# Forgetting attention: two row maxima and the normalisation ahead of the last state steps, three weight blocks behind them, and the last state group's inputs in two pairs

## The chip, the cores and the metric

One core of one Trainium2 chip runs the whole program. The metric is device time in microseconds of one execution. All matrix work is on the tensor engine (PE), vector arithmetic on the vector engine (DVE), activations and many copies on the scalar engine (ACT), and the sync engine (SP) issues the DMA transfers. Every engine works through its own list of instructions in order, and waits on semaphores.

## What the reference computes

The program is a chain of four transformer layers over 256 tokens of width 1024. The change touches the mixer of the third, which runs a softmax attention with forgetting (8 heads of 64) beside a state space scan (S5, width 512), and multiplies both by one output matrix:

```python
def fox_s5_mixer(x, w_in, f_bias, ..., d_skip, w_glu, b_glu, w_out):
    z = x @ w_in
    q, k, v, f_logit, u = jnp.split(z, ...)
    att = forgetting_attention(q, k, v, f_logit + f_bias)     # softmax(q k^T/8 + c_i - c_j) v
    y = s5_scan(u, ..., d_skip)                               # complex scan, then C h + d_skip * u
    y = jax.nn.gelu(y)
    y = y * jax.nn.sigmoid(y @ w_glu + b_glu)
    return jnp.concatenate([att, y], axis=-1) @ w_out
```

Behind it come a residual, a layer norm, and a mixture of experts.

## The kernel before, in words

**Weights.** Matrices come in pieces of 128 by 1024 floats (512 KB), numbered through the program. SP loads piece n into one of four raw slots, and waits for that until the low part of piece n-4 is made. ACT copies it, rounded, to a high slot (`hi_to(n)`, one CAST of WH from WR; there are five such slots), and DVE makes the remainder (`lo_to(n)`, one TENSOR_TENSOR of WL from WR and WH). The order of ACT and DVE work around these is written out by hand: `filled(u)` first makes pieces up to three beyond the one in use, then waits for a PSUM bank.

The stage "fox" has pieces 0 to 23 of its own: 0 to 15 are input weights, 16 to 23 the rows of `w_out`. When they are named here by number, the count is from `FIRST["fox"]`. `down(s, ...)` multiplies the activations GH/GL of row block s with piece 16+s into four banks, 12 matmuls. Blocks 0 to 3 are the attention's, 4 to 7 the state part's.

**Attention.** There are 16 units (head, query tile), i = 0 to 15. For each PE scores into a bank, DVE takes the maximum of the rows (L2664), ACT the exponential (L1465), PE transposes it (`turn`, L882), ACT copies that back (`keep_turned`, L1556), and PE multiplies with the values (`fox_value`). Behind unit 15 DVE normalises (`normalize_out`, L2408 and two products), PE transposes the result (`turn_out`, L892), and ACT and DVE split it into GH and GL (`high_out`, `low_out`).

**State part.** Four groups i = 0 to 3. `s5_in(i)` on PE makes the inputs of a group in four banks (two pairs), which ACT copies (L1730, L1731). DVE turns them by an angle, scans and turns them back, in the generator `s5_states`: seven steps a group, 28 in all, each taken by one `next(states)`. The steps of a group are: the two products with the cosine; the first sine product and sum; the second sine product and difference, with the skip term (`s5_skip`) of the group before; four scans; four scans; two products into RS and ACC; two into AR, which signal `s_grot`. `s5_out(i)` on PE waits for that signal and makes the group's output.

**The end of the stage.** `s5_skip` adds d_skip * u to an output. ACT applies gelu to groups 0 to 2 in one instruction, makes the high parts up to piece 23, and applies gelu to group 3. PE multiplies with the gate's weights (`gate_units`): groups 0 to 2 first, group 3 (8 matmuls) behind it. ACT takes the sigmoid, DVE multiplies, ACT and DVE split into GH and GL, and PE runs the blocks 4 to 7 (`down_by_tiles`).

**Banks.** Scores, state inputs and outputs take turns in a ring of four PSUM banks, in the order of PE's program. A bank is taken again once its last reader is through.

Of the kernel before, what the change touches and what calls it, by code (L numbers as in the profile page):

```python
# [21 lines left out]
LOOK = 3  # L22
# [114 lines left out]
PLAN, FIRST = weight_plan()  # L137
# [225 lines left out]
def build(nc, a, out):  # L363
    ctx = ExitStack()
    with ctx:
# [124 lines left out]
        GLB, at = {}, 0  # L490
# [45 lines left out]
        fot = AR[:, r.at + 256:r.at + 1280]  # L536
# [101 lines left out]
        def _(e):  # L638
# [111 lines left out]
                half_of_tokens(u, 0)  # L750
                half_of_tokens(u, 1)

            def down(i, made, first, last, bank_of=lambda b: 4 + b):

                n, h, l = piece()
                e.wait_ge(s_gl.sem, made)
                for b in range(4):
                    ts, fs = slice(b // 2 * P, b // 2 * P + P), slice(b % 2 * 512, b % 2 * 512 + 512)
                    t = mm3(bank(bank_of(b)), gh[:, i, ts], gl[:, i, ts], h[:, fs], l[:, fs], first, last)
                    if last:  # L760
                        t.then_inc(s_y.sem, 1)
                if not last:
                    t.then_inc(s_used.sem, 1)
# [374 lines left out]
                e.wait_ge(s_t2.sem, 8 * STAGE["fox"] + k + 1)  # L1138
                t = mm(bank(u.b, 0, 256, p=8), foxg[:, k, :], t2[:, k, :], k == 0, k == 7)
            t.then_inc(u.fill[0], 1)  # L1140
            def s5_in(i):
                for pair in range(2):
                    us = [use(("s5b", i, 2 * pair + x)) for x in range(2)]
                    for r in range(2):
                        for x, u in enumerate(us):
                            rows = slice(64 * pair + 32 * x, 64 * pair + 32 * x + 32)
                            t = mm(bank(u.b, r * 256, r * 256 + 256), BT[r][rows, i, :], fuf[rows, i, :], True, True)
                            if r:
                                t.then_inc(u.fill[0], 1)
# [41 lines left out]

            fox_scores(0)
            for i in range(18):
                if i in (4, 11):
                    s5_in(2 + i // 7)
                if i < 15:
                    fox_scores(i + 1)
                if i >= 2:
                    if (i - 2) % 8 == 0:
                        e.wait_ge(*ring.uses["fv", (i - 2) // 8].free)  # L1200
                    fox_value(i - 2)
                if 1 <= i <= 16:
                    turn(16 + i - 1, fSb[(i - 1) % 3], (i - 1) % 2 + 1, (s_exp.sem, 16 + i))
                if i == 0:
                    features(("fq", 1), "fox")
                if i == 2:
                    features(("fk", 1), "fox")
                if i == 5:
                    tokens(("fv", 1))
                if i in (3, 9, 15):  # L1210
                    s5_out((i - 3) // 6)
            busy(3)
            turn_out("fox", fot, 4)
            busy(4)

# [7 lines left out]
                    if 3 in ks:  # L1223
                        t.then_inc(u.fill[0], 1)

            for s in range(2):
                down(s, GLB["fox"] + 1, s == 0, False)
            us = [use(("glu", s)) for s in range(2)]
            e.wait_ge(s_glu.sem, 32)
            e.wait_ge(s_ys.sem, 1)  # L1230
            gate_units(us, range(3))
            down(2, GLB["fox"] + 2, False, False)
            s5_out(3)
            down(3, GLB["fox"] + 2, False, False)
            e.wait_ge(s_ys.sem, 2)
            gate_units(us, [3])
            down_by_tiles(range(4, 8), [GLB["fox"] + 3 + x // 2 for x in range(4)], True)
            layer_norm_and_logits(0)

# [218 lines left out]
        def _(e):  # L1458
# [262 lines left out]
                A.wait()  # L1721
                A(act(x, x, ACTF.Ln, bias=1.0), s_lsa)

            def s5_in(i):
                for jj in range(4):
                    u = ring.uses["s5b", i, jj]
                    filled(u)
                    if i and jj == 0:
                        e.wait_ge(s_s5r.sem, i)
                    e.copy(Br[:, jj, :], bank(u.b, 0, 256))  # L1730
                    A.frees(e.copy(Bi[:, jj, :], bank(u.b, 256, 512)), u)  # L1731
# [36 lines left out]
            for i in range(17):  # L1768
                if i < 16:
# [6 lines left out]
                    if i >= 3:  # L1776
                        e.wait_ge(*pring.uses["pt", 16 + i - 3].fill)
                    A(act(sbf, bank(u.b, 0, n), ACTF.Exp, bias=mx[:, c:c + 1], accum=den[:, c:c + 1]), s_exp)
                if i in (4, 11):
                    s5_in(2 + i // 7)  # L1780
                if i:
                    keep_turned(16 + i - 1, (i - 1) % 2 + 1, fpts[(i - 1) % 2], 16 + i - 2)
                if i == 0:
# [198 lines left out]
        def _(e):  # L1982
# [628 lines left out]
            V(ts(fcf, fcw, -1.0, None, ALU.mult), s_cpos)  # L2611
            def s5_skip(i):
                u = ring.uses["s5y", i]
                filled(u)
                V.frees(stt(YS[:, i, :], fuf[:, i, :], par("s5d", i, 1), bank(u.b, 0, 256), ALU.mult, ALU.add), u)

            def s5_states():
# [41 lines left out]
            for i in range(16):  # L2659
# [2 lines left out]
                u = ring.uses["fs", i]  # L2662
                filled(u)
                V(e.tensor_reduce(mx[:, c:c + 1], bank(u.b, 0, n), AX.X, ALU.max, negate=True), s_neg)  # L2664
                next(states, None)
            lo_to(FIRST["fox"] + 18)
            next(states, None)
            normalize_out(fot, 32)
            lo_to(FIRST["fox"] + 19)
            low_out("fox")  # L2670
            next(states, None)
            next(states, None)
            for n in range(FIRST["fox"] + 20, FIRST["fox"] + 23):
                next(states, None)
                lo_to(n)
            for _ in states:
                pass
            lo_to(FIRST["fox"] + 23)
            s5_skip(3)
            for s in range(2):  # L2680
                lo_to(ring.uses["glu", s].piece + LOOK)
                e.wait_ge(*ring.uses["glu", s].free)
                V(tt(fqf[:, 2 * s:2 * s + 2, :], fqf[:, 2 * s:2 * s + 2, :], YS[:, 2 * s:2 * s + 2, :], ALU.mult), s_glum)
                low_of(GLB["fox"] + 3 + s, 4 + 2 * s, 6 + 2 * s, fqf[:, 2 * s:2 * s + 2, :])
# [495 lines left out]
```

## Time and profile before

| what | value |
|---|---|
| three runs, median (lowest to highest) | 1477.95 us (1476.88 to 1481.66) |
| the profiled execution, its own time | 1481.88 us |
| its span in the trace | 1480.1 us |
| PE busy | 1412.4 us, 95% |
| DVE busy | 1172.9 us, 79% |
| ACT busy | 827.7 us, 56% |

The shares of busy time are averages over stages of very different kinds. The stretch that the change touches lies between 838 and 900 us of the span. How long something took there, and what ended each wait, is read from the order of instructions in time.

### The profile page before, as it was taken

The numbers are of one execution on the slowest core, as the hardware profiler recorded it, in microseconds if no ns is written. First come the engines' busy times: TensorE is split into PE (matmuls) and PEld (weight loads), VectorE is DVE, ScalarE is ACT, GpSimd is POOL, SyncE is SP. The second block draws the span as 40 slices with busy tenths as digits, with TensorE's granted clock in tenths as the row PEclk, the third lists the DMA queues.
The fourth block names the chain that finished last, engine by engine and source line by source line (L and its number), as shares of the span: only waits on it lengthen the run. The fifth ranks groups of instructions, "written<-read, shape, count | busy, mean of one in ns | idle before, by whom it ended". The sixth has DMA issues, their size and how long they took to land.

```text
span 1480.1 us, 22953 instructions
## 1 busy us (share of the span) xinstructions
PE 1412.4 (95%) x8738; PEld 1245.1 (84%) x8738; DVE 1172.9 (79%) x1800; ACT 827.7 (56%) x1210; POOL 1.2 (0%) x5
## 2 busy tenths in 40 slices
PE   7889899999999999999999889999999999999997
PEld 7888788888898979999979668888879998888886
DVE  4898787887865757598569887799988966879997
ACT  1442444544544445444676435788866564678874
POOL 0000000000000000000000000000000000000000
PEclk7899999999999999999999999999999999999999
DMA  9973389997575524655735124899954544589992
GB/s 367 323 297 108 122 307 345 342 331 255 180 227 163 187 70 143 199 180 180 212 111 147 58 92 179 301 384 368 385 197 115 165 121 156 180 322 374 372 380 78
DMA packets 184480, 333.76 MB, mean 225 GB/s; under 512 B 13340, under 2 KB 127796, under 8 KB 184372
## 3 DMA queue, kind: packets, MB, share of 16 engines
q1 hardware_dynamic: 184372, 332.31, 64.7%
q8 instruction: 70, 1.15, 0.3%
q14 instruction: 38, 0.31, 0.1%
HBM read 331.18 MB, written 1.09 MB: 224 GB/s over the span
## 4 chain that ended last, share of the span: by engine, by line
PE 76%; DVE 13%; DMA 4%; ACT 3%; issue 3%; SPq 1%; DVEq 0%; ACTq 0%
PE PSA L645 14%; PE PSA L647 14%; PE PSA L646 14%; PE PSA L642 13%; PE PSB L645 5%; PE PSB L646 5%; PE PSB L647 5%; PE PSB L642 4%; DVE WL L1996 2%; DMA WR<-ffn_w_in 2%; DVE ACC L1993 2%; DVE T L1996 1%; DVE AR L1996 1%; DMA WR<-hyb_w_in 1%; ACT WH L1475 1%
## 5 line engine op out<-in xcount | busy, mean ns | idle before, releaser
L1996 DVE TENSOR_TENSOR WL<-WR,WH 128x1024 fp32r<-128x1024 f32 x352 | 422.4, 1219 | 100.4 <-ACT WH L1475 99.7
L1475 ACT CAST WH<-WR 128x1024 fp32r<-128x1024 f32 x352 | 357.0, 1048 | 114.4 <-DMA WR<-hyb_w_in 45.0
L645 PE MATMUL PSA<-XHL,WH 128*128 128x256 f32 x976 | 282.7, 290 | 8.4 <-ACT T L1464 2.2
L647 PE MATMUL PSA<-XHL,WL 128*128 128x256 f32 x976 | 277.1, 284 | 0.0
L646 PE MATMUL PSA<-XHL,WH 128*128 128x256 f32 x976 | 277.1, 284 | 0.0
L645 PEld LDWEIGHTS PSA<-XHL,WH 128*128 128x128 f32 x976 | 188.0, 193 | 13.9 <-issue 5.2
L1996 DVE TENSOR_TENSOR WL<-AR,WH 128x1024 fp32r<-128x1024 f32 x152 | 178.4, 1219 | 14.1 <-ACT WH L1475 14.1
L646 PEld LDWEIGHTS PSA<-XHL,WH 128*128 128x128 f32 x976 | 188.2, 193 | 0.9 <-issue 0.5
L647 PEld LDWEIGHTS PSA<-XHL,WL 128*128 128x128 f32 x976 | 188.1, 193 | 0.0
L645 PE MATMUL PSB<-WH,GH 128*128 128x512 f32 x400 | 159.5, 399 | 5.0 <-DVE GL L1996 5.0
L646 PE MATMUL PSB<-WL,GH 128*128 128x512 f32 x400 | 156.7, 392 | 0.0
L647 PE MATMUL PSB<-WH,GL 128*128 128x512 f32 x400 | 156.5, 391 | 0.0
L1475 ACT CAST WH<-AR 128x1024 fp32r<-128x1024 f32 x152 | 151.5, 1049 | 4.0 <-PE PSA L647 4.0
L642 PE MATMUL PSA<-XHL,WH 128*128 128x512 f32 x336 | 118.8, 397 | 2.1 <-ACT T L1464 1.6
L645 PE MATMUL PSA<-WH,XHL 128*128 128x256 f32 (+1 forms) x352 | 116.2, 330 | 3.9 <-DVE AR L1993 2.7
L647 PE MATMUL PSA<-WH,XHL 128*128 128x256 f32 (+1 forms) x352 | 113.5, 322 | 0.0
L646 PE MATMUL PSA<-WL,XHL 128*128 128x256 f32 (+1 forms) x352 | 113.3, 322 | 0.0
L645 PEld LDWEIGHTS PSB<-WH,GH 128*128 128x128 f32 x400 | 75.5, 189 | 23.9 <-issue 8.5
L642 PE MATMUL PSA<-XHL,WL 128*128 128x256 f32 x336 | 94.3, 281 | 0.0
L647 PEld LDWEIGHTS PSB<-WH,GL 128*128 128x128 f32 x400 | 75.5, 189 | 16.3
L646 PEld LDWEIGHTS PSB<-WL,GH 128*128 128x128 f32 x400 | 75.6, 189 | 15.1 <-issue 0.5
L1464 ACT ACTIVATE AR<-PSA 128x256 f32<-128x256 f32 (+1 forms) x71 | 31.1, 441 | 94.8 <-PE PSA L647 94.8
(276 smaller groups left out, 2372.4 us busy)
## 6 DMA issues: line engine op xcount, KB each, us to landing
AR<-moe_w_gate_up SPq DMA_DIRECT2D x96, 512.0 KB, 6.4
WR<-ffn_w_in SPq DMA_DIRECT2D x88, 512.0 KB, 4.9
WR<-moe_w_gate_up SPq DMA_DIRECT2D x64, 512.0 KB, 6.4
AR<-ada_w SPq DMA_DIRECT2D x59, 512.0 KB, 9.2
AR<-moe_w_down SPq DMA_DIRECT2D x56, 512.0 KB, 6.8
WR<-ffn_w_out SPq DMA_DIRECT2D x44, 512.0 KB, 4.2
WR<-att_w_qkv SPq DMA_DIRECT2D x36, 512.0 KB, 5.0
AD<-ada_w SPq DMA_DIRECT2D x34, 512.0 KB, 6.3
```

What stands on the lines that cost most here:

```text
L642: return e.matmul(o, l, r, start=start, stop=stop, skip_group_check=skip)
L645: e.matmul(o, lh, rh, start=start, stop=False, skip_group_check=True)
L646: e.matmul(o, lh, rl, start=False, stop=False, skip_group_check=True)
L647: return e.matmul(o, ll, rh, start=False, stop=stop, skip_group_check=True)
L1464: return e.activation(o, i, f, bias=bias, scale=scale)
L1475: A(e.copy(hi_slot(m), raw_slot(m)), s_hi)
L1993: return e.scalar_tensor_tensor(out=o, in0=i, scalar=s, in1=j, op0=op0, op1=op1)
L1996: return e.tensor_tensor(o, i, j, op)
```

## The change

It edits the programs of PE, ACT and DVE between unit 11 of this attention and the end of the stage.

```diff
 PE
-                if i in (4, 11):
-                    s5_in(2 + i // 7)
+                if i == 4:
+                    s5_in(2)
+                if i in (11, 12):
+                    s5_in(3, (i - 11,))
...
-                if i in (3, 9, 15):
+                if i in (3, 9):
                     s5_out((i - 3) // 6)
-            busy(3)
+            s5_out(2)
             turn_out("fox", fot, 4)
...
-            for s in range(2):
-                down(s, GLB["fox"] + 1, s == 0, False)
+            for s in range(3):
+                down(s, GLB["fox"] + 1 + s // 2, s == 0, False)
...
             gate_units(us, range(3))
-            down(2, GLB["fox"] + 2, False, False)
             s5_out(3)
-            down(3, GLB["fox"] + 2, False, False)
-            e.wait_ge(s_ys.sem, 2)
-            gate_units(us, [3])
+
+            def last_gate_units():
+                e.wait_ge(s_ys.sem, 2)
+                gate_units(us, [3])
+
+            down(3, GLB["fox"] + 2, False, False, between=last_gate_units)
 ACT
-                if i in (4, 11):
-                    s5_in(2 + i // 7)
+                if i == 4:
+                    s5_in(2)
+                if i in (11, 12):
+                    s5_in(3, (i - 11,))
 DVE
             def s5_skip(i):
                 u = ring.uses["s5y", i]
-                filled(u)
+                e.wait_ge(*u.fill)
...
-                next(states, None)
+                if i < 14:
+                    next(states)
+            next(states)
+            normalize_out(fot, 32)
             lo_to(FIRST["fox"] + 18)
-            next(states, None)
-            normalize_out(fot, 32)
-            lo_to(FIRST["fox"] + 19)
+            next(states)
             low_out("fox")
-            next(states, None)
-            next(states, None)
-            for n in range(FIRST["fox"] + 20, FIRST["fox"] + 23):
-                next(states, None)
-                lo_to(n)
             for _ in states:
                 pass
+            lo_to(FIRST["fox"] + 19)
+            s5_skip(3)
             lo_to(FIRST["fox"] + 23)
-            s5_skip(3)
             for s in range(2):
-                lo_to(ring.uses["glu", s].piece + LOOK)
```

The DVE list from the maximum of unit 14 to the low parts of the attention's result, as it stood. AR<-T,AR is the last step of group 2 (the one that signals `s_grot`), T<-T,AR and T<-T are the first steps of group 3, RECIPROCAL and AR<-PSB,SM are the normalisation:

```order
L2664 TENSOR_REDUCE SM<-PSA 128x1 [waits s_bank1_filled]
L1996 TENSOR_TENSOR AR<-T,AR 128x1024 [waits s_neg_made]
L1996 TENSOR_TENSOR AR<-T,AR 128x1024
L2664 TENSOR_REDUCE SM<-PSA 128x1 [waits s_bank2_filled]
L1996 TENSOR_TENSOR T<-T,AR 128x1024 [waits s_neg_made,s_bank2_free]
L1996 TENSOR_TENSOR T<-T,AR 128x1024 x2
L1996 TENSOR_TENSOR T<-T 128x1024 [waits s_dve_step]
L2408 RECIPROCAL SM<-SM 128x8 [waits s_exp_made]
L1996 TENSOR_TENSOR AR<-PSB,SM 128x512 [waits s_dve_step,s_val_made]
...
L1996 TENSOR_TENSOR WL<-WR,WH 128x1024 [waits s_hi_made]
L1996 TENSOR_TENSOR GL<-PSA,GH 128x512 [waits s_gh_made,s_bank0_filled]
```

And in the changed kernel (its lines are numbered eight higher):

```order
L2672 TENSOR_REDUCE SM<-PSA 128x1 [waits s_bank1_filled]
L2672 TENSOR_REDUCE SM<-PSA 128x1 [waits s_bank2_filled]
L2004 TENSOR_TENSOR AR<-T,AR 128x1024 [waits s_neg_made]
L2004 TENSOR_TENSOR AR<-T,AR 128x1024
L2416 RECIPROCAL SM<-SM 128x8 [waits s_exp_made]
L2004 TENSOR_TENSOR AR<-PSB,SM 128x512 [waits s_dve_step,s_val_made]
...
L2004 TENSOR_TENSOR T<-T,AR 128x1024 [waits s_ot_made,s_bank3_free]
L2004 TENSOR_TENSOR T<-T,AR 128x1024
L2004 TENSOR_TENSOR GL<-PSA,GH 128x512 [waits s_gh_made,s_bank0_filled]
```

The two maxima now follow each other, the normalisation has one step of the state part ahead of it instead of three, and the low part of piece 19 (WL) is gone from this place.

Further down the same list, from the scans of group 3 to the product with the sigmoid, as it stood. T<-AR,T are the scans, RS and ACC the last step but one, AR<-T,AR the last, and AR<-AR,PR,PSA is the skip term of group 3:

```order
L2002 SCALAR_TENSOR_TENSOR T<-AR,T 128x256 x7
L1996 TENSOR_TENSOR WL<-WR,WH 128x1024 [waits s_hi_made]
L1996 TENSOR_TENSOR RS<-T,AR 128x1024 [waits s_lo_made]
L1993 SCALAR_TENSOR_TENSOR ACC<-T,AR 128x1024
L1996 TENSOR_TENSOR WL<-WR,WH 128x1024 [waits s_hi_made]
L1996 TENSOR_TENSOR AR<-T,AR 128x1024 [waits s_lo_made]
L1996 TENSOR_TENSOR AR<-T,AR 128x1024
L1996 TENSOR_TENSOR WL<-WR,WH 128x1024 [waits s_hi_made] x2
L1993 SCALAR_TENSOR_TENSOR AR<-AR,PR,PSA 128x256 [waits s_bank0_filled]
L1996 TENSOR_TENSOR AR<-AR 128x512 [waits s_bank2_free]
```

And in the changed kernel:

```order
L2010 SCALAR_TENSOR_TENSOR T<-AR,T 128x256 x7
L2004 TENSOR_TENSOR RS<-T,AR 128x1024 [waits s_dve_step]
L2001 SCALAR_TENSOR_TENSOR ACC<-T,AR 128x1024
L2004 TENSOR_TENSOR AR<-T,AR 128x1024 [waits s_dve_step]
L2004 TENSOR_TENSOR AR<-T,AR 128x1024
L2004 TENSOR_TENSOR WL<-WR,WH 128x1024 [waits s_hi_made]
L2001 SCALAR_TENSOR_TENSOR AR<-AR,PR,PSA 128x256 [waits s_bank0_filled]
L2004 TENSOR_TENSOR WL<-WR,WH 128x1024 [waits s_hi_made] x4
L2004 TENSOR_TENSOR AR<-AR 128x512 [waits s_bank2_free]
```

The low parts of pieces 20 and 21 leave the middle of the steps, and one low part (now piece 19) stands between the last step and the skip term, with four behind it (20 to 23) instead of two ahead.

On PE the last block of the attention's rows, `down(3)`, is split around the gate's last products (PSA<-AR):

```order
-L645 MATMUL PSB<-WH,GH 128x512
-L646 MATMUL PSB<-WL,GH 128x512
-L647 MATMUL PSB<-WH,GL 128x512
-L645 MATMUL PSB<-WH,GH 128x512
-L646 MATMUL PSB<-WL,GH 128x512
-L647 MATMUL PSB<-WH,GL 128x512
 L642 MATMUL PSA<-AR 128x256 [waits s_ys_made]
 L642 MATMUL PSA<-AR 128x256 x3
+L645 MATMUL PSB<-WH,GH 128x512
+L646 MATMUL PSB<-WL,GH 128x512
```

Six of its twelve matmuls come behind the gate's products now.

## Rows read from the trace of the kernel before

**Rows 1.** The page: the span, and busy time by engine
```profile
span 1480.1 us, 22953 instructions
...
PE 1412.4 (95%) x8738; PEld 1245.1 (84%) x8738; DVE 1172.9 (79%) x1800; ACT 827.7 (56%) x1210; POOL 1.2 (0%) x5
```

**Rows 2.** Timeline of DVE: start us, us, instruction, [idle before <-releaser]
```profile
841.48 2.44 DVE L2002 TENSOR_TENSOR_SCAN T<-AR,T 128x256 f32<-128x256 f32 x4
845.50 0.29 DVE L2664 TENSOR_REDUCE SM<-PSA 128x1 f32<-128x128 f32 x1 [1.59 <-PE PSA L642]
...
850.77 0.28 DVE L2664 TENSOR_REDUCE SM<-PSA 128x1 f32<-128x128 f32 x1
...
853.36 0.42 DVE L2664 TENSOR_REDUCE SM<-PSA 128x1 f32<-128x256 f32 x1
853.89 3.50 DVE L1996 TENSOR_TENSOR T<-T,AR 128x1024 f32<-128x1024 f32 x3
...
859.76 0.69 DVE L1996 TENSOR_TENSOR AR<-PSB,SM 128x512 f32<-128x512 f32 x1
860.37 1.22 DVE L1996 TENSOR_TENSOR WL<-WR,WH 128x1024 fp32r<-128x1024 f32 x1
861.68 1.29 DVE L1996 TENSOR_TENSOR GL<-PSA,GH 128x512 fp32r<-128x512 f32 x2
```

**Rows 3.** Timeline of PE over the same stretch and the end of the stage
```profile
842.24 2.08 PE L642 MATMUL PSA<-AR,AD 32*128 32x256 f32 x8 [2.09 <-ACT AR L1465]
...
853.59 0.74 PE L642 MATMUL PSA<-RS,AD 128*32 128x256 f32 x8 [0.91 <-DVE AR L1996]
...
856.83 0.69 PE L642 MATMUL PSB<-AR 128*128 128x64 f32 x2
...
858.21 0.66 PE L642 MATMUL PSB<-AR 128*128 128x64 f32 x4 [0.46 <-ACT AR L1556]
...
860.05 1.11 PE L892 MATMUL PSA<-CT,AR 128*128 128x128 f32 x8
...
882.50 1.89 PE L642 MATMUL PSA<-AR 128*128 128x256 f32 x8
886.65 0.47 PE L645 MATMUL PSB<-WH,GH 128*128 128x512 f32 x1 [2.26 <-DVE GL L1996]
```

**Rows 4.** Timeline of DVE, the end of the state part
```profile
875.23 2.36 DVE L1996 TENSOR_TENSOR AR<-T,AR 128x1024 f32<-128x1024 f32 x2
...
879.78 0.47 DVE L1993 SCALAR_TENSOR_TENSOR AR<-AR,PR,PSA 128x256 f32<-128x256 f32 x1
```

**Rows 5.** Timeline of ACT, the end of the stage
```profile
880.29 0.42 ACT L1464 ACTIVATE AR<-AR 128x256 f32<-128x256 f32 x1 [2.86 <-DVE AR L1993]
880.73 1.28 ACT L1464 ACT_TABLE_LOAD   x1
883.56 1.70 ACT L1464 ACTIVATE AR<-PSA,PR 128x256 f32<-128x256 f32 x4 [1.55 <-PE PSA L642]
```

**Rows 6.** One line's DMA issues: time from issue to landing
```profile
DMA to landing us min/median/max: 3.4/4.2/4.7
```

**Rows 7.** DMA issues between 880 and 890 us: KB each, us to landing
```profile
WR<-moe_w_gate_up SPq DMA_DIRECT2D x4, 512.0 KB, 8.6
```

**Rows 8.** Timeline of ACT behind the stage: cast, table load, activation
```profile
913.17 1.05 ACT L1475 CAST WH<-WR 128x1024 fp32r<-128x1024 f32 x1
914.24 1.28 ACT L1464 ACT_TABLE_LOAD   x1
915.53 0.21 ACT L1464 ACTIVATE SM<-SM 128x8 f32<-128x8 f32 x1
```

**Rows 9.** PE alone by stretch: busy, granted clock, DMA share, GB/s
```profile
854.00:856.00 2.00, 2.00 (x27) 0.50 0.03 8
...
888.00:890.00 2.00, 2.00 (x7) 0.53 1.04 420
890.00:892.00 2.00, 2.00 (x7) 0.61 0.65 264
```

More of the change, by code:

```diff
@@ L751, in tokens, with down @@
                 half_of_tokens(u, 1)
-            def down(i, made, first, last, bank_of=lambda b: 4 + b):
+            def down(i, made, first, last, bank_of=lambda b: 4 + b, between=None):
                 n, h, l = piece()
@@ L757, in down @@
                 for b in range(4):
+                    if b == 2 and between:
+                        between()
                     ts, fs = slice(b // 2 * P, b // 2 * P + P), slice(b % 2 * 512, b % 2 * 512 + 512)
@@ L1140, in _, with s5_in @@
             t.then_inc(u.fill[0], 1)
-            def s5_in(i):
-                for pair in range(2):
+            def s5_in(i, pairs=(0, 1)):
+                for pair in pairs:
                     us = [use(("s5b", i, 2 * pair + x)) for x in range(2)]
@@ L1722, in log_sigmoid, with s5_in @@
                 A(act(x, x, ACTF.Ln, bias=1.0), s_lsa)
-            def s5_in(i):
-                for jj in range(4):
+            def s5_in(i, pairs=(0, 1)):
+                for jj in range(2 * pairs[0], 2 * pairs[-1] + 2):
                     u = ring.uses["s5b", i, jj]
```

## The prediction

> **What bounds the kernel now.** I read the page first: PE is busy for 95% of a span of 1480.1 us [rows 1], so all that a reordering can win is waiting time of PE, and only where nothing else makes it up. The trace in order of time then shows that the touched stretch is one of the few where PE is not the bound. From the row maxima to the output of state group 3 it is DVE's list that runs without a gap, and PE, ACT and DMA wait for it. Three places matter. Before the maximum of unit 12 DVE itself sat idle for 1.59 us, for scores of PE [rows 2], and PE had been held by the second pair of state inputs, 2.09 us, until an exponential of ACT freed a bank [rows 3]. Between the maximum of unit 15 at 853.36 and the end of the normalisation at 860.45 (859.76 + 0.69) DVE ran four long state instructions [rows 2]. And after the last step of group 3 (875.23 + 2.36 = 877.59 [rows 4]) comes the chain skip term, gelu, gate, sigmoid, product, GL, until PE starts the state rows of the output matrix at 886.65 after 2.26 us of idling [rows 3]. From there on PE has work in a row, so I take 886.65 as the time that must move: what lies behind it (sums, layer norm, the experts' loads, which wait for the sums) starts from it and moves along. What does not arrive at 886.65 is worth nothing.
>
> **Step 1, two pairs of inputs.** The scores of unit 12 no longer queue behind the second pair. They need a bank whose reader is the skip term of group 1, done just before the scans that start at 841.48. These scans end at 843.92, and the maximum can follow at once instead of at 845.50: 1.6 us off DVE's list [rows 2]. The second pair runs beside the next scans, and PE and ACT have slack there. The lower bound is 0 (the scores late for another reason).
>
> **Step 2, maxima and normalisation.** With step 1 the maximum of unit 14 starts at 850.77 - 1.6 = 849.2, that of unit 15 at 849.5, 3.9 us earlier than 853.36 [rows 2]. What ends the attention then is the ping-pong of exponential, transposition, copy and value product for units 14 and 15. It took from 853.36 to 858.87 (858.21 + 0.66), and the output of group 2 stood inside it with 3.24 us (853.59 to 856.83) [rows 2, 3], part of it beside the exponential. I put the last value product at 854.0, 4.5 us after the maximum, and the end of the normalisation at 854.6, against 860.45.
>
> **Step 3, what this meets.** The output of group 2 now starts behind the value products, at 854.0, and the transposition of the result queues behind it. It took 3.24 us before, at the lower of PE's clock levels (granted 0.50 from 854 to 856 [rows 9]); half of that, 1.6 us, is my estimate for the full level. So the transposition starts at 857.2 or 855.6, and GL follows 1.63 us behind its start (860.05 to 861.68) [rows 2, 3]: at 858.8 or 857.3, against 861.68. The step gains **2.9 to 4.4 us**. The pair of products that DVE does between normalisation and GL (two of 1.2 us) fits into this wait and is free.
>
> **Step 4, from GL to the last step of group 3.** Before: 861.68 to 877.59, 15.9 us [rows 2, 4]. Two low parts leave it (2 x 1.2 us, as WL at 860.37); two state products of the same size, which had stood ahead of the normalisation, enter it. The length stays at 15.9 us, so the last step ends 2.9 to 4.4 us earlier: at 874.7 or 873.2.
>
> **Step 5, what is given back.** Piece 19's low part is now made behind this step (1.2 us; the output of group 3 on PE covers it, since the skip term started 2.19 us after the last step also before, 877.59 to 879.78 [rows 4]). But the load of piece 23 waits for exactly that low part, and ACT must cast piece 23 before it may apply gelu to group 3. Before, that load had been issued some 16 us ahead, and only the skip term held ACT (the wait of 2.86 us [rows 5]). Now the gelu starts at: last step + 1.2 (low part) + landing + 1.05 (cast [rows 8]) + 0.1. Loads of these rows landed in 3.4 to 4.7 us, median 4.2 [rows 6]; I take 3.5, nearest to the low end, since nothing else is in flight then. That is 5.8 us behind the last step, against 880.29 - 877.59 = 2.7 before [rows 4, 5]: **3.1 us lost**, 4.3 with a landing of 4.7. The four low parts behind the skip term (4.6 us) end a little after the cast of piece 23, at 881, about when the first sigmoids are through, and cost nothing; if they ended later, the product would wait one for one.
>
> **Step 6, the split of down(3).** Before, gelu started at 880.29, the gate's last products only at 882.50, since PE had to finish twelve matmuls, and the sigmoid at 883.56; 886.65 is 3.09 us behind the sigmoid [rows 3, 5]. Now the gate can start with the end of gelu, and the sigmoid with the end of the table load: gelu 0.42, load 1.28, then 3.09, together 4.8 us instead of 6.36. **1.55 us gained.** Behind the gate six matmuls are left, inside that 3.09.
> A rule of the Trainium skill weighs on this step. Here a table load of 1.28 us is followed by its activation without a gap (914.24, then 915.53 [rows 8]). "ScalarE: Activation LUTs", section "What ACT_TABLE_LOAD costs", adds a drain of about 1.38 us to each switch; the load before was hidden by PE, and it is not now, so by the page the step would gain 0.2 us and the whole change 0.7. I go by the row.
>
> **Sum.** 2.9 to 4.4, less 3.1, plus 1.55: 1.35 to 2.85, and with the late landing 0.1 to 1.6. I take 2.1. The profiled execution's own time of 1481.88 would become 1479.8. It lies 3.9 above the median of the runs; on the median 1477.95 the same 2.1 gives **1475.8 us**. A measurement of this kernel can tell about 0.3% from no change, which is 4.4 us: the forecast is a gain too small to be told.
>
> **The rivals.**
> *Forecast* (0.55): 1475.8, its own range 1474.2 to 1477.8.
> *PE's clock stays up* (0.2). From 888 to 892 us the granted clock was 0.53 and 0.61 [rows 9], partly the lower level (1.2 GHz), after the wait of 2.26 us [rows 3]; that costs 2 x 0.47 + 2 x 0.39 = 1.7 us of PE's work. If the new order keeps the full level there and during the output of group 2, the gain is 4.4 - 3.1 + 1.55 + 1.7 = 4.55: 1473.4. For it: the last wait of PE may shrink. Against it: PE now also waits ahead of the output of group 3 and of the gate's last products, and waits of 0.91 and 2.26 us stood before the two slow stretches [rows 3]. By "TensorE: Matmul & The Clock Gate", section "What's actually happening", of the Trainium skill, idling sends the clock down, which speaks for the slow stretch staying; the trace agrees that it did so before.
> *Nothing arrives* (0.15). The scores of unit 12 are late anyway, the output of group 2 runs at the lower level and the load lands in 4.7 us: the gain of steps 1 to 3 is used up by step 5. 1478.
> *Piece 23 decides for the worse* (0.1), the case on the other side. Four loads of the same size, issued together, took 8.6 us [rows 7]. If this one took as long, gelu would start 5.1 us later than I put it: 2.1 - 5.1 = -3.0, 1481.0. The change turns into a loss from a landing of 5.6 us on. Against it: the queue is empty at that time.
>
> **How the numbers follow.** The predicted time is the forecast's. The range of 8 in 10 reaches from just under the faster case to beyond the case where nothing arrives, as the spread of the runs shown (1476.88 to 1481.66) also asks: 1472.6 to 1480.0. Faster by over 0.3% needs the faster case and a little more than its own size, 0.15; slower by over 0.3% needs more than the whole price of the last rival, 0.05; within 0.3% is the rest, 0.80.
>
> **What would show it.** Step 1: no idling of DVE before the maximum of unit 12. Step 2: the two last maxima back to back. Step 3: PE's output of group 2 right ahead of the transposition, GL 3 to 4 us earlier against the maximum of unit 11. Step 5: ACT's cast of piece 23 released by its DMA, right ahead of the last gelu. Step 6: sigmoid directly behind the table load. Wrong is the prediction if the cast does not wait, if the transposition waits for something else than the output of group 2, or if the gain at the state rows is lost in the experts' stage.

## The result

The changed kernel took 1487.6 us (median of 8 runs, 1485.56 to 1490.01), the kernel before beside it 1480.71 us (8 runs, 1476.88 to 1484.66). The ratio is 1.0045, with a 95% interval of 1.0031 to 1.0058: slower by 6.7 us, where 2.1 us faster was forecast. Every ratio below is that of a kernel's runs to those of the kernel before, and a number of microseconds said to be by the ratio is worked out from it. The profiled execution's span is 1487.9 us against 1480.1 [rows 1].

```profile
span 1487.9 us, 22941 instructions
...
PE 1419.8 (95%) x8732; PEld 1250.5 (84%) x8732; DVE 1173.1 (79%) x1800; ACT 827.2 (56%) x1210; POOL 1.2 (0%) x5
```

The shares are the same as before. The time in order has to be read. First the DVE of the changed kernel (start us, us, instruction, [idle before <-releaser]), from the first state steps of group 1 on. AR<-AR,PR,PSA is the skip term (the one at 821.29 of group 0, that at 885.04 of group 3), RS and ACC the last step but one of a group.

```profile
815.40 1.23 DVE L2004 TENSOR_TENSOR T<-T 128x1024 f32<-128x1024 f32 x1
821.29 0.48 DVE L2001 SCALAR_TENSOR_TENSOR AR<-AR,PR,PSA 128x256 f32<-128x256 f32 x1 [4.67 <-PE PSA L642]
821.69 2.35 DVE L2004 TENSOR_TENSOR WL<-WR,WH 128x1024 fp32r<-128x1024 f32 x2
...
828.53 0.42 DVE L2672 TENSOR_REDUCE SM<-PSA 128x1 f32<-128x256 f32 x1 [1.81 <-PE PSA L642]
...
837.31 0.42 DVE L2672 TENSOR_REDUCE SM<-PSA 128x1 f32<-128x256 f32 x1 [1.16 <-PE PSA L642]
...
851.23 0.27 DVE L2672 TENSOR_REDUCE SM<-PSA 128x1 f32<-128x128 f32 x1
...
854.36 0.42 DVE L2672 TENSOR_REDUCE SM<-PSA 128x1 f32<-128x256 f32 x1 [0.53 <-PE PSA L642]
...
858.10 0.42 DVE L2672 TENSOR_REDUCE SM<-PSA 128x1 f32<-128x256 f32 x1 [0.71 <-PE PSA L642]
...
866.84 1.29 DVE L2004 TENSOR_TENSOR GL<-PSA,GH 128x512 fp32r<-128x512 f32 x2 [1.39 <-ACT GH L1568]
...
880.54 2.36 DVE L2004 TENSOR_TENSOR AR<-T,AR 128x1024 f32<-128x1024 f32 x2
882.81 1.22 DVE L2004 TENSOR_TENSOR WL<-WR,WH 128x1024 fp32r<-128x1024 f32 x1
885.04 0.48 DVE L2001 SCALAR_TENSOR_TENSOR AR<-AR,PR,PSA 128x256 f32<-128x256 f32 x1 [1.01 <-PE PSA L642]
```

The same place in the kernel before, which the rows ahead of the prediction do not show:

```profile
813.82 2.35 DVE L1996 TENSOR_TENSOR WL<-WR,WH 128x1024 fp32r<-128x1024 f32 x2
818.58 0.48 DVE L1993 SCALAR_TENSOR_TENSOR AR<-AR,PR,PSA 128x256 f32<-128x256 f32 x1 [2.40 <-PE PSA L642]
```

Here a loss starts that the prediction does not have. The skip term of group 0 waits for an output of PE. Before, DVE made two low parts first and then idled 2.40 us; now it idles 4.67 us and makes the two low parts behind the wait. The place is far ahead of unit 11, where the part of the change that I costed begins: that the change lies between unit 11 and the end of the stage, and the touched stretch between 838 and 900 us, as was said ahead of the prediction, is wrong. It follows from one line of the diff, `filled(u)` turned into a bare wait in `s5_skip`, which serves all four groups. In the two lists of instructions the place reads, before and now:

```
L1996 TENSOR_TENSOR WL<-WR,WH 128x1024 [waits s_hi_made] x2
L1993 SCALAR_TENSOR_TENSOR AR<-AR,PR,PSA 128x256 [waits s_bank1_filled]

L2001 SCALAR_TENSOR_TENSOR AR<-AR,PR,PSA 128x256 [waits s_bank1_filled]
L2004 TENSOR_TENSOR WL<-WR,WH 128x1024 [waits s_hi_made] x2
```

PE of the changed kernel, at the inputs of group 2, the output of group 2, the transposition, the output of group 3, the gate's last products, the second half of `down(3)` and the first state rows:

```profile
824.84 2.08 PE L642 MATMUL PSA<-AR,AD 32*128 32x256 f32 x8 [2.55 <-ACT AR L1471]
...
862.18 1.08 PE L642 MATMUL PSA<-RS,AD 128*32 128x256 f32 x8
...
865.24 1.09 PE L894 MATMUL PSA<-CT,AR 128*128 128x128 f32 x8
...
883.05 0.64 PE L642 MATMUL PSA<-RS,AD 128*32 128x256 f32 x8 [1.60 <-DVE AR L2004]
...
889.46 3.78 PE L642 MATMUL PSA<-AR 128*128 128x256 f32 x8 [2.89 <-ACT AR L1470]
892.68 0.99 PE L645 MATMUL PSB<-WH,GH 128*128 128x512 f32 x1
...
895.50 0.47 PE L645 MATMUL PSB<-WH,GH 128*128 128x512 f32 x1
```

PE alone by stretch (us, busy, granted clock, DMA share, GB/s):

```profile
822.00:826.00 4.00, 1.45 (x10) 0.71 0.48 140
826.00:830.00 4.00, 4.00 (x20) 0.50 0.36 122
...
850.00:854.00 4.00, 4.00 (x16) 0.50 0.00 0
...
890.00:894.00 4.00, 4.00 (x11) 0.50 0.94 251
```

PE waited 2.55 us at the inputs of group 2, for the exponential of unit 4, whose maximum now stands behind the two low parts (823.96), and worked at its lower clock level (granted 0.50) from 826 to 830; a second such stretch lay at 850, and a third from 890, on the gate's products, which took 3.78 us instead of 1.89 [rows 3].

ACT of the changed kernel at the end of the stage:

```profile
888.04 1.05 ACT L1481 CAST WH<-WR 128x1024 fp32r<-128x1024 f32 x1 [11.97 <-DMA WR<-even_w_out]
888.99 0.41 ACT L1470 ACTIVATE AR<-AR 128x256 f32<-128x256 f32 x1
889.42 1.28 ACT L1470 ACT_TABLE_LOAD   x1
891.57 0.84 ACT L1470 ACTIVATE AR<-PSA,PR 128x256 f32<-128x256 f32 x2 [0.87 <-PE PSA L642]
```
SP's queue in the same kernel, where the load of piece 23 is issued:
```profile
884.06 0.34 SPq L2969 DMA_DIRECT2D WR<-even_w_out  x1
```

The load of piece 23, issued at 884.06 behind the low part of piece 19, held the cast until 888.04 and the gelu behind it, as forecast.

**One clock for all traces.** The skip term of group 0 starts when PE has finished the output that it waits for, and up to that output PE's list is the same in every kernel here. That time lies between 816.5 and 822.3 us in the profiled executions. I count everything behind it from it. The table gives what the traces show, in us: DVE's idle time ahead of that skip term, then the start of the maxima of units 7, 12 and 15, of GL, the end of the last state step, the skip term of group 3, its gelu, the first sigmoid, the first state rows on PE, and the first product of the residual (XT) on DVE. Each row is one execution, the profiled one. Where the last two maxima are one row of the trace, the second is counted back from its end.

| kernel | idle | max 7 | max 12 | max 15 | GL | last step ends | skip 3 | gelu | sigmoid | state rows | XT |
|---|---|---|---|---|---|---|---|---|---|---|---|
| before | 2.40 | 11.33 | 26.92 | 34.78 | 43.10 | 59.01 | 61.20 | 61.71 | 64.98 | 68.07 | 74.76 |
| changed | 4.67 | 16.02 | 29.94 | 36.81 | 45.55 | 61.61 | 63.75 | 67.70 | 70.28 | 74.21 | 79.26 |
| e1 | 2.42 | 11.33 | 25.25 | 32.15 | 40.89 | 56.95 | 59.08 | 62.72 | 65.30 | 68.82 | 73.88 |
| e2 | 4.67 | 14.90 | 30.49 | 38.35 | 46.66 | 62.57 | 64.76 | 65.27 | 68.54 | 71.63 | 76.71 |
| e3 | 2.40 | 11.33 | 25.25 | 33.72 | 42.03 | 57.94 | 60.13 | 60.64 | 63.87 | 66.96 | 73.60 |
| e4 | 2.40 | 11.33 | 25.25 | 31.32 | 38.56 | 54.63 | 56.77 | 57.28 | 61.85 | 64.94 | 72.53 |
| e5 | 2.42 | 11.33 | 25.25 | 32.06 | 40.79 | 56.85 | 58.99 | 59.50 | 61.43 | 66.14 | 72.70 |
| e6 | 4.69 | 15.82 | 30.43 | 38.30 | 47.89 | 63.80 | 65.99 | 66.50 | 69.73 | 72.82 | 79.51 |
| e7 | 2.42 | 11.33 | 25.24 | 32.09 | 40.82 | 56.88 | 59.02 | 59.54 | 62.81 | 66.17 | 72.73 |
| e8 | 2.42 | 11.33 | 26.92 | 32.54 | 39.66 | 55.72 | 57.86 | 62.01 | 64.48 | 68.40 | 73.49 |
| e9 | 4.67 | 13.60 | 29.19 | 37.05 | 45.36 | 61.28 | 63.47 | 63.97 | 67.22 | 70.31 | 76.96 |
| e10 | 2.40 | 11.33 | 25.25 | 32.16 | 40.90 | 56.96 | 59.10 | 59.62 | 61.53 | 65.11 | 70.19 |
| e11 | 2.42 | 11.32 | 25.24 | 31.32 | 39.46 | 55.51 | 57.65 | 58.17 | 60.08 | 63.67 | 68.74 |
| e12 | 2.40 | 11.34 | 25.25 | 30.69 | 40.86 | 56.91 | 59.06 | 59.57 | 61.48 | 65.07 | 70.13 |

The changed kernel is 16.02 - 11.33 = 4.69 us behind at the maximum of unit 7, has won 2.66 of them back at unit 15, and is 2.6 behind at the last state step. Between the skip term of group 3 and its gelu, where the load of piece 23 is waited for, it loses another 3.4, and at the state rows it is 74.21 - 68.07 = 6.14 behind. At XT it is 4.50 behind (79.26 - 74.76), because the state rows themselves took longer in the kernel before: 6.69 us from their start to XT, with a granted clock of 0.53 and 0.61 [rows 9], against 5.05. Of the 7.8 us between the two spans another 2.7 lie ahead of the skip term, where nothing differs in the lists, and 0.6 behind XT.

### The profile page after: what moved, and what is told of

The parts are those of the page before. It is cut to its first block, busy times and chain, and to the rows that moved or that the text cites. A ratio compares the mean times of both kernels' runs of the same rounds, so it can differ in the third digit from the quotient of the medians.

```text
span 1487.9 us, 22941 instructions
## 1 busy us (share of the span) xinstructions
PE 1419.8 (95%) x8732; PEld 1250.5 (84%) x8732; DVE 1173.1 (79%) x1800; ACT 827.2 (56%) x1210; POOL 1.2 (0%) x5
## 4 chain that ended last, share of the span: by engine, by line
PE 71%; DVE 15%; DMA 6%; ACT 4%; issue 4%; SPq 1%; DVEq 0%; ACTq 0%
PE PSA L645 13%; PE PSA L642 13%; PE PSA L647 12%; PE PSA L646 12%; PE PSB L645 5%; PE PSB L646 5%; PE PSB L647 5%; PE PSB L642 4%; DVE WL L2004 3%; DMA WR<-ffn_w_in 2%; DVE ACC L2001 2%; DMA AD<-ada_w 2%; DVE T L2004 1%; ACT WH L1481 1%; DVE AR L2004 1%
```

## The experiments

The theory after the result, S: the bare wait in `s5_skip` loses the filling of a wait (DVE no longer makes low parts while it would wait anyway), and with it PE's clock for a while. Its rivals: C, the two programs differ by chance of clock and placing; O, the new order around units 14 and 15 costs. Each kernel is compared with the kernel before on the same chip.

**e1, the filling given back.**
```diff
 # the changed kernel
-                e.wait_ge(*u.fill)
+                if i < 3:
+                    filled(u)
+                else:
+                    e.wait_ge(*u.fill)
```


> The changed kernel, with one line given back: the skip term of groups 0 to 2 first makes the low parts up to three pieces ahead again, and then waits for its bank (group 3 keeps the bare wait). Theory S (the skip's lost filling): in the changed kernel DVE idles 4.67 us at 816.6 us of its span with two low parts (2.35 us) undone that the kernel before made inside this very wait, and everything up to unit 7 moves from 2.7 to 7.4 us late, part of it PE at the lower clock level after a wait of 2.55 us. Then this kernel loses the 4.7 us, and keeps the 1.4 us that the rest of the change won between unit 7 and the first state rows: ratio to before 0.998 to 1.000, DVE idle before the skip term of group 0 about 2.4 us. Rival C (chance of clock and placing: the two programs differ in where slow stretches fall, nothing in this stage does it): ratio stays at 1.004 to 1.005. Rival O (the new order behind unit 13 costs): ratio also stays near 1.004.

Measured: 0.9993 (0.9979 to 1.0008), inside the expected range. The wait is at 2.42 us again, unit 7 where it was before. C and O both wanted 1.004 and fall.

**e2, the skip edit alone.**
```diff
 # the kernel before
-                filled(u)
+                e.wait_ge(*u.fill)
```


> The kernel before, with only the skip edit: s5_skip waits for its bank without making low parts first. Nothing else is changed. Theory S: slower by 4 to 5 us, ratio 1.003 to 1.0035, the same idle time of 4.7 us on DVE before the skip term of group 0, two low parts behind it. Rival C or O: within 1.000 plus or minus 0.001.

Measured: 1.0034 (1.0023 to 1.0046), 5.0 us slower by the ratio (the two medians differ by 4.2). The same idle time stands in front of the skip term, and unit 7 comes 3.57 us late. S holds, from both sides.

**e3, the two pairs alone**, `s5_in` with pairs as the changed kernel has it.
```diff
 # the kernel before, PE and ACT alike
-                if i in (4, 11):
-                    s5_in(2 + i // 7)
+                if i == 4:
+                    s5_in(2)
+                if i in (11, 12):
+                    s5_in(3, (i - 11,))
```

> The kernel before, with only the inputs of group 3 in two pairs (units 11 and 12, PE and ACT). By my prediction DVE wins the 1.6 us before the maximum of unit 12; but in the changed kernel 0.53 us of idling came before the maximum of unit 13 and 0.71 before that of unit 15, so I expect 0.3 to 1 us of the 1.6 to be left: ratio 0.999 to 1.000. If pairs only move the stall, the maximum of unit 15 stands where it stood.

Measured: 0.9984 (0.9975 to 0.9994), a little lower than the 0.999 to 1.000 expected, and clear of no change. Unit 12 comes 1.67 us earlier, unit 15 only 1.06, and XT 1.16.

**e4, gelu ahead of the cast.**
```diff
 # e1, ACT
-            hi_to(FIRST["fox"] + 23)
+            hi_to(FIRST["fox"] + 22)
             e.wait_ge(*ring.uses["s5y", 3].free)
             A(act(YS[:, 3, :], YS[:, 3, :], ACTF.Gelu_apprx_tanh), s_ys)
+            hi_to(FIRST["fox"] + 23)
```


> As e1, and ACT applies the gelu of group 3 ahead of the cast of piece 23 instead of behind it. Theory D (the load of piece 23, issued only behind the low part of piece 19, holds gelu): in the changed kernel the cast waited for its DMA until 888.04 and gelu started at 888.99, while the skip term was ready at 885.5: gelu can start 3.4 us earlier, so the first state rows start 2 to 3 us earlier than in e1: ratio to before about 0.997 to 0.998. Rival: the low part of piece 23, which DVE makes ahead of the product with the sigmoid, then waits as long as gelu did, and nothing is won: ratio as e1.

Measured: 1.0002 (0.9988 to 1.0015). ACT's rows (start us, us, instruction, [idle]):
```profile
877.46 0.42 ACT L1470 ACTIVATE AR<-AR 128x256 f32<-128x256 f32 x1 [9.48 <-DVE AR L2002]
879.67 1.05 ACT L1481 CAST WH<-WR 128x1024 fp32r<-128x1024 f32 x1 [1.79 <-DMA WR<-even_w_out]
880.74 1.28 ACT L1470 ACT_TABLE_LOAD   x1
882.03 1.57 ACT L1470 ACTIVATE AR<-PSA,PR 128x256 f32<-128x256 f32 x4
```
I had expected 0.997 to 0.998. Half of the reason is that the wait for the load went from gelu to the cast and the table load behind it: the gap between gelu and sigmoid grew from 2.6 us in e1 to 4.6. Of the 3.1 us that gelu won against the skip term (0.51 us behind it instead of 3.64), 1.6 are left at the state rows (8.17 us behind the skip term, 9.74 in e1). The other half is PE's clock. The state rows follow a wait of 3.54 us and start at the lower level:
```profile
885.12 0.77 PE L645 MATMUL PSB<-WH,GH 128*128 128x512 f32 x1 [3.54 <-DVE GL L2005]
```
From them to XT it took 7.59 us, in e1 5.06. So what was won at the state rows is gone at XT.

**e5, piece 19 early again.**
```diff
 # e1, DVE
             next(states)
+            lo_to(FIRST["fox"] + 19)
             low_out("fox")
             for _ in states:
                 pass
-            lo_to(FIRST["fox"] + 19)
             s5_skip(3)
```


> As e1 (the changed kernel with the low parts ahead of the skip term given back), and the low part of piece 19 stands ahead of the attention's low parts again, as in the kernel before, instead of behind the last state step. In e1 DVE idled 1.42 us right there, waiting for GH, so the low part is free there; and the load of piece 23 is issued some 15 us earlier. Theory D (the load of piece 23 held gelu and with it the gate): cast of piece 23 no longer waits, gelu starts 0.5 us behind the skip term instead of 3.64, the gate's last products run at once, and the first state rows start 2 to 3.5 us earlier than in e1, counted from the skip term of group 0: ratio to before 0.996 to 0.998. Rival P (PE's own work or its clock bounds the end: gate and six matmuls): less than 1 us earlier, ratio as e1 (0.999).

Measured: 0.9993 (0.9978 to 1.0007). The load no longer holds anything (gelu 0.51 us behind the skip term, 3.64 in e1), and the low part fitted into DVE's wait for GH (GL at 40.79 and 40.89). The state rows start 2.7 us earlier, as expected, but the ratio, expected at 0.996 to 0.998, shows nothing of it. In the trace XT comes only 1.2 us earlier than in e1: the state rows stood behind a wait of PE of 2.50 us and took 6.56 us to XT, 5.06 in e1. And the sigmoid is done early while the product behind it is not. DVE's rows:
```profile
878.81 4.63 DVE L2004 TENSOR_TENSOR WL<-WR,WH 128x1024 fp32r<-128x1024 f32 x4
883.35 0.69 DVE L2004 TENSOR_TENSOR AR<-AR 128x512 f32<-128x512 f32 x1
```
The four low parts (pieces 20 to 23) now end last.

**e7, e5 with down(3) in one piece again.**
```diff
 # e5, PE
-            down(3, GLB["fox"] + 2, False, False, between=last_gate_units)
+            down(3, GLB["fox"] + 2, False, False)
+            e.wait_ge(s_ys.sem, 2)
+            gate_units(us, [3])
```

> As e5, with the fourth block of weight rows in one piece again, ahead of the gate's last products. What the split is worth once gelu is in time: my step 6 says 1.55 us at most, so 1 to 1.5 us slower than e5 (ratio 0.001 higher), the gate's last products 1.5 us later against the gelu. If PE's matmuls behind the gate cost as much as those ahead of it: the same as e5.

Measured: 0.9998 (0.9984 to 1.0011); state rows at 66.17 against 66.14. The sigmoid came 1.4 us later and nothing followed from it, since the low parts ended last in both. The split is worth nothing in this order, where the low parts hide it; I had expected 1 to 1.5 us. In the order of e10, further down, where the product starts at 62.90, it might be worth something, and that was not run.

**e8, e1 without the pairs.**
```diff
 # e1, PE and ACT alike
-                if i == 4:
-                    s5_in(2)
-                if i in (11, 12):
-                    s5_in(3, (i - 11,))
+                if i in (4, 11):
+                    s5_in(2 + i // 7)
```

> As e1 without the two pairs: the inputs of group 3 are all made at unit 11 again. What is left is the order of maxima, normalisation and low parts and the split. From e1 (maximum of unit 12 1.67 us earlier than before, counted from the skip term of group 0) and e3 (pairs alone, 1.5 us earlier) I expect the pairs to carry what e1 wins: DVE idles 1.6 us before the maximum of unit 12 again, everything up to the gate 1 to 1.6 us later than in e1, ratio to before 1.000 to 1.001. If the other edits won by themselves, ratio below 0.999.

Measured: 1.0015 (1.0001 to 1.0029). The 1.59 us of idling ahead of unit 12 are back, but by unit 15 only 0.4 us are left of it, and GL comes 1.2 us earlier than in e1: in e1 the output of group 2 met a granted clock of 0.59 and 0.56 (854 to 858), here 1.00. The ratio, like that of e3, speaks for the pairs and this trace against them; what they bring beside the other edits stays open.

**e6 and e9, the clock's part in the skip edit.**
```diff
 # e2, PE; 11 in e6, 5 in e9
+                if i == 4:
+                    for _ in range(5):
+                        mm(bank(4, 256, 512), ident, CT[:, 0:256], True, True)
                 if i in (4, 11):
                     s5_in(2 + i // 7)
```


> As e2 (the kernel before with only the skip edit), and PE runs 11 matmuls of no use (into columns of bank 4 that are begun later) while it waits for the inputs of group 2, where it idled about 2.5 us. They cost 2.5 us of PE's time in a wait of the same length. It tells apart what the lost filling costs as lateness of DVE (2.3 us) and what as PE's clock behind the wait: in e2 the maximum of unit 7 came 14.9 us behind the skip term of group 0, in the kernel before 11.3. With the clock kept up I expect about 13.6 or less... if the slow stretch is cause of a part: no half clock at 827 us, ratio 1.002 to 1.003. If the clock has no part: as e2, 1.0034 or a little more.

e6 measured 1.0033 (1.0019 to 1.0047), a little above the 1.002 to 1.003 expected. Its 11 matmuls took 5.0 us and overran the wait, so it told nothing of the clock.

> As e6, with 5 matmuls of no use instead of 11: e6's took 5.0 us and overran the wait, so it could not tell clock from lateness. Five take 2.3 us and fit into the 2.55 us that PE idled in e2. In e2 the maximum of unit 7 came 14.90 us behind the skip term of group 0, in the kernel before 11.33, a loss of 3.57, of which 2.27 is two low parts of DVE behind its wait instead of in it. If the half clock at 827 us of e2 is the rest, unit 7 comes at 13.6 to 14.0 and there is no slow stretch there. If it is not the clock, 14.9 again. The ratio will hardly tell (1.0025 to 1.0034).

e9 measured 1.0005 (0.9988 to 1.0021). PE's rows in e9:
```profile
820.10 2.43 PE L642 MATMUL PSB<-CT 128*128 128x256 f32 x10
822.46 1.13 PE L642 MATMUL PSA<-AR,AD 32*128 32x256 f32 x8
```
and its stretches:
```profile
824.00:828.00 4.00, 3.98 (x32) 1.00 0.55 184
828.00:832.00 4.00, 4.00 (x35) 1.00 0.00 0
```
The clock stays at its full level (1.00), where e2 had 0.68 from 826 to 830. Unit 7 comes at 13.60: 2.27 us late by the two low parts, which is exactly what the idle time grew by (4.67 - 2.40), and 1.30 us of e2's 3.57 were the clock's. In the changed kernel the low stretch was longer, and took 2.42 (16.02 - 13.60).

The ratio says more than the trace. Expected at 1.0025 to 1.0034, it lies 0.0029, or 4.3 us, below that of e2, and the two intervals do not meet; but at the state rows e9's trace is only 1.32 us ahead of e2's, and at XT 0.25 behind it. The profiled execution of e9 took 1487.48 us, against a median of 1482.74. So by the ratios the clock's part in e2's loss may be most of it, and the split above holds for the traces alone.

**e10, the low part of piece 23 last.**
```diff
 # e5, DVE
-            lo_to(FIRST["fox"] + 23)
+            lo_to(FIRST["fox"] + 22)
             for s in range(2):
                 e.wait_ge(*ring.uses["glu", s].free)
                 V(tt(fqf[:, 2 * s:2 * s + 2, :], ..., ALU.mult), s_glum)
                 low_of(GLB["fox"] + 3 + s, 4 + 2 * s, 6 + 2 * s, fqf[:, 2 * s:2 * s + 2, :])
+            lo_to(FIRST["fox"] + 23)
```


> As e5, and the low part of piece 23 stands behind the two low parts of the gated state instead of ahead of the first product. In e5 gelu was in time (0.51 us behind the skip term), but the product with the sigmoid began only at 883.35, when DVE's four low parts were through, 1.65 us behind the second sigmoid. Theory L (now these low parts are the bound): the product 1.1 us earlier, the first state rows at about 65 us behind the skip term of group 0 instead of 66.1, ratio 0.0007 lower than e5 (0.998 to 0.999). Rival: the state rows then wait for piece 23 and the end does not move.

Measured: 0.9969 (0.9956 to 0.9982): **faster than the kernel before**, 4.6 us by the ratio and 2.8 by the medians (1478.51 against 1481.28); the changed kernel's ratio was 1.0045. The gain is larger than the 0.998 to 0.999 that I had expected. The state rows start at 65.11, 1.03 earlier than in e5; the low part of piece 23 runs behind them, and PE never waits for it:
```profile
886.98 1.22 DVE L2004 TENSOR_TENSOR WL<-WR,WH 128x1024 fp32r<-128x1024 f32 x1
890.31 0.69 DVE L2177 SCALAR_TENSOR_TENSOR XT<-XT,PSB 128x512 f32<-128x512 f32 x1 [2.11 <-PE PSB L647]
```
XT comes 2.51 us earlier than in e5. The other 1.48 us are PE's clock: behind a shorter wait, of 1.39 us instead of 2.50, the state rows ran at the full level (granted 1.00):
```profile
885.23 0.47 PE L645 MATMUL PSB<-WH,GH 128*128 128x512 f32 x1 [1.39 <-DVE GL L2004]
```

**e11, e10 with PE kept busy ahead of the state rows.**
```diff
 # e10, PE
             down(3, GLB["fox"] + 2, False, False, between=last_gate_units)
+            busy(3)
             down_by_tiles(range(4, 8), [GLB["fox"] + 3 + x // 2 for x in range(4)], True)
```

> As e10, and PE runs three matmuls of no use (1.4 us) in its wait between the last attention rows and the first state rows. In e4 and e5 these rows began with 3.4 us or more at the lower clock, which costs 1.7 us. If the last wait alone made the clock fall, the slow stretch is gone and the first sum of the residual comes up to 1.7 us earlier than in e10. If the earlier waits ahead of the output of group 3 did it, nothing changes.

Measured: 0.9975 (0.9959 to 0.999). From the first state rows to XT 5.07 us, in e10 5.08: there was no low stretch in either, so the question was not put. Inconclusive. Its state rows start 1.44 us earlier than e10's, as the output of group 2 ran at the full level; the low part of piece 19 no longer fitted into a wait there, and from the maximum of unit 15 to GL it took 8.14 us, in e4 7.24.

**e12, e10 with PE kept busy at unit 11.**
```diff
 # e10, PE
+                def beside():
+                    for _ in range(3 if i == 11 else 0):
+                        mm(bank(4, 320, 512), ident, CT[:, 0:192], True, True)
+
+                beside()
                 if i in (11, 12):
                     s5_in(3, (i - 11,))
+                beside()
```

> As e10, and PE runs three short matmuls of no use (128 by 192, about 1 us together, into columns of bank 4 that are begun later) in each of its two waits at unit 11, before and behind the first pair of inputs of group 3 (1.34 and 1.02 us of idling in e10). In e1, e5 and e10 the granted clock fell for 10.2 us right behind them (from 841.8 us on in e10), and the scores of units 13 to 15 and the output of group 2 ran at the lower level; in e4 and e11 the stretch was 6.8 us, and GL came 1.4 to 2.3 us earlier, counted from the skip term of group 0 (38.56 and 39.46 against 40.9). Theory K (these waits let the clock fall, and the low stretch costs the gain of step 3): no or a shorter low stretch there, GL at 38.5 to 39.5, the ratio up to 0.0015 lower than that of e10 (0.9955 to 0.997). Rival: the clock falls all the same behind the waits that are left, ratio as e10 (0.997), or 0.0005 higher for the matmuls that overrun a wait.

Measured: 0.9986 (0.997 to 1.0003). PE alone by stretch, e12:
```profile
842.00:846.00 4.00, 3.16 (x24) 1.00 0.00 0
846.00:850.00 4.00, 2.08 (x13) 1.00 0.00 0
850.00:854.00 4.00, 3.04 (x21) 0.71 0.01 4
854.00:858.00 4.00, 4.00 (x36) 0.50 0.71 246
```
and e10:
```profile
842.00:846.00 4.00, 3.30 (x15) 0.50 0.00 0
846.00:850.00 4.00, 4.00 (x20) 0.50 0.00 0
```
The scores ran at the full level and unit 15 came 1.5 us earlier; the low stretch then fell on the output of group 2 (854 to 858), and GL stood where it had stood (40.86 and 40.90). The rival was right in the mechanism: the clock falls behind the waits that are left. The ratio came out above what either side had expected.

## Why the prediction was wrong, by its steps

**What failed is a term that was not there.** My sum began at unit 11. The sum put the edit in `s5_skip` at nothing, and gave no reason for it. In its parts, the skip term appears only as group 1's ("done just before the scans that start at 841.48") and group 3's; the edit has no line of its own, though it was in the diff that I quoted. For groups 1 and 2 it changes nothing. For group 0 it moves two low parts from inside a wait for PE to behind it. The trace's row for that wait was at hand (2.40 us of idling behind two low parts at 813.82), and 4.67 - 2.40 = 2.27 us of it was to be had by reading. In the changed kernel it made 4.69 us by unit 7. None of my rivals held it. e1 and e2 settle this from both sides; e9 splits e2's loss by unit 7 into 2.27 us of lateness and 1.30 us of PE's clock behind its 2.55 us wait, and the 4.69 us into 2.27 and 2.42.

**The rest of the sum.** With the missing term given back, e1 shows what my steps were worth. The last state step ends 59.01 - 56.95 = 2.06 us earlier (forecast 2.9 to 4.4), step 5 gives back 5.77 - 2.70 = 3.07 (3.1), and step 6 wins 0.26 (1.55): the state rows start 0.75 us later than before, not 2.1 earlier. Steps 1 to 3 and step 6 were sized too high.

**Step 1 (pairs, 1.6 us).** Right at its place: unit 12 comes 1.67 us earlier in e1 and e3. Too much further on: in the changed kernel DVE waited 0.53 and 0.71 us for scores ahead of units 13 and 15, PE working at the lower level from 850 on.

**Step 2 (unit 15 3.9 us earlier).** e1 shows 34.78 - 32.15 = 2.6. The two maxima were not back to back there; the scores of unit 15 were 0.74 us late. In e4 and e11, where the low stretch was shorter, it was 3.5; in e8, without the pairs, 2.2.

**Step 3 (GL 2.9 to 4.4 us earlier).** 2.2 in e1, 3.6 in e11, 4.5 in e4. The mechanism was right: the output of group 2 stands between value products and transposition, and PE's level there decides. It took 1.87 us at the full level (e4, 855.28 to 857.15; I had put 1.6) and 3.06 in the changed kernel (862.18 to 865.24; I had put 3.24). From the maximum of unit 15 to GL it was 7.24 us in e4 and 8.74 in e1, whose lists are the same there. The change also took out `busy(3)`, matmuls of no use ahead of the transposition; I put no price on that, and no run tells it.

**Step 4 (15.9 us from GL to the last state step).** Right: 15.9 us before, 16.06 in the changed kernel and in e1.

**Step 5 (3.1 us given back by the load of piece 23).** Right: gelu came 5.77 us behind the last step in e1 and 6.09 in the changed kernel, against 5.8 forecast and 2.70 before. The load took at most 3.98 us there (884.06 to 888.04). Its second half was wrong: that four low parts ahead of the product "cost nothing" holds only while gelu is late. With gelu in time they ended last (e5), and e10 won the state rows 1.03 us by moving one.

**Step 6 (1.55 us gained).** Hardly found. From gelu to state rows I had put 4.8 us; e1 took 6.10, the changed kernel 6.51, before 6.36. The gate's last products ran at the lower level behind PE's wait of 2.89 us (3.78 us instead of 1.89), and the six matmuls of `down(3)` behind them came ahead of the state rows. e7 shows the split to be worth nothing in the order of e5, even with gelu in time. The table load was followed by its activation with no gap in e4 (880.74 + 1.28, then 882.03) as in [rows 8], so the row was the right price there, and the 1.38 us more that the Trainium skill puts on a switch ("ScalarE: Activation LUTs", section "What ACT_TABLE_LOAD costs") did not appear.

**The end point.** I took the start of the state rows for the time that counts. What arrives there need not arrive at XT, since the clock of the state rows themselves varied. From their start to XT it took 5.05 to 5.09 us in the changed kernel, e1, e2, e8, e10, e11 and e12, and 6.56 to 7.59 in the kernel before, e3, e4, e5, e6, e7 and e9. The rival "PE's clock stays up" asked for the full level there and at the output of group 2; the changed kernel had it at the state rows and not at the output of group 2, and lost more behind the new waits.

**What stays open.** Counted in the traces, the changed kernel loses 6.14 us up to the state rows and 4.50 up to XT, e2 3.56 and 1.95, while the ratios say 6.7 and 5.0. The lower clock on the state rows in the profiled execution of the kernel before, which e2 and the changed kernel had not, closes most of the gap, but for e2 not all. How much of the loss is the clock's, e9's ratio and its trace answer differently. The stretch ahead of the skip term varied by nearly 6 us among executions of equal lists, and I have not found whether the changed kernel is more often on its late side.

## What to carry to other kernels

When a helper changes, walk every caller of it through the list of instructions before pricing anything: a call that looks like a mere wait may be what fills the wait. Where an engine waits for another, what stands ahead of the waiting instruction is free up to the length of the wait, and what stands behind it is not; ask of each moved piece on which side of the next wait it now lies. And follow a piece of preparation to its last consumer: here a low part that cost nothing in itself released a load, the load a cast, and the cast an activation that ended the stage.

## What the runs showed of the hardware

A wait of PE of 2.55 us cost more than itself: behind it the granted clock fell to 0.50, and the clock's part by unit 7 was 1.3 us in e2 and 2.4 us in the changed kernel, in one execution of each. Five useless matmuls in the wait kept it at 1.00 (e9). But filling one pair of waits in e12 only moved the low stretch to the next place, and bought nothing that the ratio shows.

Ahead of the state rows the profiled executions give a longer list. Behind waits of 2.26 to 3.54 us the state rows began at or soon fell to the lower level in seven of eight (the kernel before, e3, e4, e5, e6, e7 and e9; not e2, whose wait was 2.26 us too). Behind waits of 1.39 us or less (the changed kernel with none, e1, e8, e10, e12) they never did. With the lower level it took 1.5 to 2.5 us longer to XT. By "TensorE: Matmul & The Clock Gate", section "What's actually happening", of the Trainium skill, idling lowers the clock and activity releases it; the traces agree, with the addition that in which of several waits it falls differed between kernels whose lists there are the same (e1 and e4).
